# A hybrid decoder step on one Trainium2 core: RWKV preparation in a written-out pipeline, compression copies on GpSimd, the feed-forward program of TensorE without its loop

## What is computed

```python
def rwkv7_mix(xr, wkv0, lw):              # xr: token-shifted projection, p + (previous p - p) * mu
    r, k, v = xr[..., :o1], xr[..., o1:o2], xr[..., o2:o3]
    wl, al, gl = xr[..., o3:o4], xr[..., o4:o5], xr[..., o5:]
    w_log = -jax.nn.softplus(-(lw['w0'] + jnp.tanh(wl) @ lw['w2']).astype(f32)) - 0.5
    decay = jnp.exp(-jnp.exp(w_log))
    a = jax.nn.sigmoid((lw['a0'] + al @ lw['a2']).astype(f32))
    g = jax.nn.sigmoid(gl) @ lw['g2']
    kk = heads(k * lw['k_k'])
    kk = kk / jnp.maximum(jnp.sqrt(jnp.sum(kk * kk, axis=-1, keepdims=True)), 1e-12)
    kf = heads(k * (1.0 + (a - 1.0) * lw['k_a']))
    ...                                   # the recurrence uses r, decay, kf, v, kk, kk * a
    bonus = jnp.sum(rf * kf * lw['r_k'].astype(f32).reshape(H_R, HEAD_DIM_R), axis=-1, keepdims=True) * vf

def compress(rows, lw):                   # rows of the cache in chunks of 16, two chunks to a block
    part = jnp.einsum('bcjehd,esjdf->bcsehf', chunks, w1.reshape(2, R, D_CMP, HEAD_DIM, PHI_HIDDEN))
    h = sum(part[:, s:s + n_blk, s] for s in range(R)) + pe_term
    return jnp.einsum('bcehf,efd->bcehd', jax.nn.silu(h), lw['phi_w2'])

def channel_mix(x, lw):
    h = rms_norm(x, lw['g_ffn'])
    return x + (jax.nn.silu(h @ lw['w_gate']) * (h @ lw['w_up'])) @ lw['w_down']
```

## Time and profile before

| what | value |
|---|---|
| median of 3 runs | 4073.5 us (4072.82 to 4081.59) |
| the profiled execution | 4076.17 us |
| its span, first to last instruction | 4074.6 us |
| busy: PE, DVE, ACT, Pool | 86%, 39%, 25%, 8% |
| RWKV preparation, first DMA to the next stage's first DMA | 687.8 to 875.3 us |
| compression, first DMA to the next stage's first DMA | 1229.3 to 1709.4 us |
| feed-forward, first split of its input to the last add | 2494 to 4046 us |

### The profile page before, as it was taken

How to read it: one execution, slowest core, us unless ns; L and a number is a source line. 1 busy time by engine, 2 the same in 40 slices (tenths; PEclk the granted TensorE clock), 3 DMA queues, 4 the chain that set the end, 5 groups by cost and what they waited for, 6 DMA issues and landing times. The chain is left out here.

```text
span 4074.6 us, 69658 instructions
## 1 busy us (share of the span) xinstructions
PE 3508.3 (86%) x29755; PEld 3159.1 (78%) x29755; DVE 1577.7 (39%) x1995; ACT 1029.8 (25%) x1362; POOL 317.8 (8%) x454
## 2 busy tenths in 40 slices
PE   5999997559945888754599898999999999999998
PEld 5999996348834666632433698999999999999997
DVE  3222221953364777421255423333333333333334
ACT  4112110423213555200133323122112211211212
POOL 1000000223510000020000000000000000000000
PEclk8999996569977999787699999999999999999999
DMA  5334321344605433162300232323323332333232
GB/s 163 107 113 117 101 81 30 118 138 124 155 27 213 167 161 139 32 143 65 123 20 11 63 88 73 93 84 94 94 90 87 94 91 88 92 94 92 86 94 94
DMA packets 504916, 401.53 MB, mean 99 GB/s; under 512 B 148339, under 2 KB 457729, under 8 KB 500033
## 3 DMA queue, kind: packets, MB, share of 16 engines
q1 hardware_dynamic: 458752, 276.11, 24.4%
q0 software_dynamic: 14816, 113.89, 7.5%
q10 hardware_dynamic: 31104, 7.88, 0.9%
HBM read 359.36 MB, written 50.02 MB: 100 GB/s over the span
## 5 line engine op out<-in xcount | busy, mean ns | idle before, releaser
L2453 DVE TENSOR_TENSOR f_w_lo<-wo_raw,f_w_hi 128x2048 fp32r<-128x2048 f32 x132 | 302.5, 2292 | 820.4 <-ACT f_w_hi L2425 820.4
L53 PE MATMUL d_ps<-hh,f_w_hi 128*128 128x260 f32 x2816 | 568.4, 283 | 28.0 <-DVE xt L2477 16.3
L57 PE MATMUL d_ps<-hh,f_w_lo 128*128 128x260 f32 x2816 | 568.4, 284 | 0.0
L55 PE MATMUL d_ps<-hl,f_w_hi 128*128 128x260 f32 x2816 | 567.4, 283 | 0.0
L2425 ACT CAST f_w_hi<-wo_raw 128x2048 fp32r<-128x2048 f32 x132 | 251.9, 1908 | 994.6 <-DMA wo_raw<-in_w_gate 389.0
L53 PEld LDWEIGHTS d_ps<-hh,f_w_hi 128*128 128x128 f32 x2816 | 435.1, 189 | 30.2 <-issue 18.1
L57 PEld LDWEIGHTS d_ps<-hh,f_w_lo 128*128 128x128 f32 x2816 | 435.1, 189 | 0.0
L55 PEld LDWEIGHTS d_ps<-hl,f_w_hi 128*128 128x128 f32 x2816 | 433.8, 189 | 0.0
L53 PE MATMUL d_ps<-f_hid_hi,f_w_hi 128*128 128x260 f32 x1408 | 283.5, 282 | 0.0
L57 PE MATMUL d_ps<-f_hid_hi,f_w_lo 128*128 128x260 f32 x1408 | 283.4, 282 | 0.0
L55 PE MATMUL d_ps<-f_hid_lo,f_w_hi 128*128 128x260 f32 x1408 | 282.4, 282 | 0.0
(11 more groups left out here) (427 smaller groups left out, 5950.3 us busy)
## 6 DMA issues: line engine op xcount, KB each, us to landing
p_w<-in_w_in SPq DMA_DIRECT2D x46, 1024.0 KB, 5.6
wo_raw<-in_w_gate SPq DMA_DIRECT2D x44, 1024.0 KB, 5.6
wo_raw<-in_w_up SPq DMA_DIRECT2D x44, 1024.0 KB, 5.9
wo_raw<-in_w_down SPq DMA_DIRECT2D x44, 1024.0 KB, 5.0
wo_raw<-in_w_o SPq DMA_DIRECT2D x16, 1024.0 KB, 6.1
rk_chunks<-r_outb POOLq DMA_DIRECT2D x8, 1280.0 KB, 5.7
s_cur<-rk_chunks SPq DMA_DIRECT2D x8, 1280.0 KB, 7.1
s_one_vecs<-samp_rows SPq DMA_DIRECT2D x80, 128.0 KB, 4.9
```

The costliest lines, as they stand in the source:

```text
L53: pe.matmul(out[j], w_hi, x_hi[j], start=start, stop=False)
L55: pe.matmul(out[j], w_hi, x_lo[j], start=False, stop=False)
L57: last = pe.matmul(out[j], w_lo, x_hi[j], start=False, stop=stop)
L2453: dve.tensor_tensor(w_lo[:, s, :], w_raw[:, s, :], w_hi[:, s, :].bitcast(F32), ALU.subtract).then_inc(lo_done, 1)
```

## The change

Three stages are changed; the others stay as they are.

1. RWKV preparation: written out for the 8 pairs, with two buffers for most tiles. The token shift becomes x * (1 - mu) on ACT (in place, with the scale in `om`) and one instruction on DVE that adds mu times the row before, which a DMA now loads as a second copy shifted by one column (`prv`, `k_prev`, `lprv`). Keys of all pairs are loaded and shifted ahead of the pairs. The norms are made for all pairs at once: a product with `sel` collects the sums of squares of 16 heads on 16 partitions, one square root and one reciprocal follow, and a product with `spread` gives them back to the 128 partitions of a pair. The factor of the decay moves into the scale of the exponentials. Pool gains the second running sum (`inner`), `bvec` and a further factor of `outb`. Parameters are loaded as rows and turned by PE.
2. Compression: all copies of `arrange` are on Pool, in its own program, and the refill of a half follows its copies there.
3. Feed-forward: PE's loop over the parts is written out.

```diff
 # stage_rwkv_prep, SP
-                with sp.Fori(0, NPAIR) as i:
-                    sp.wait_ge(z_done, i * 3)
-                    sp.wait_ge(x_ready, i)
-                    for j in range(3):
-                        sp.dma_start(raw[:, j, 1:], g.proj_t[bass.ds(i * P + j * D_R, P), :]).then_inc(raw_in, 16)
-                    ...
+                for n in range(2):
+                    qs = slice(4 * n, 4 * n + 4)
+                    sp.dma_start(k_all[:, qs, :], by_pair[:, 1, qs, 0:TC]).then_inc(k_in[n], 16)
+                    sp.dma_start(k_prev[:, qs, 1:SEQ], by_pair[:, 1, qs, 0:SEQ - 1]).then_inc(k_in[n], 16)
+                    ...
+                for q in range(NPAIR):
+                    s = q % 2
+                    if q >= 2:
+                        sp.wait_ge(x_ready, q - 1)
+                    sp.dma_start(raw[:, s], by_pair[:, 0:3:2, q, 0:TC]).then_inc(rv_in[s], 16)
+                    sp.dma_start(prv[:, s, :, 1:SEQ], by_pair[:, 0:3:2, q, 0:SEQ - 1]).then_inc(rv_in[s], 16)
+                    ...
 # Pool
+                def inner(q):
+                    ...
+                    pool.tensor_tensor(cum[:, s, 1, :], cum[:, s, 0, :], sw[:, s, 0:SEQ], ALU.subtract).then_inc(cum1_ready, 1)
+                inner(0)
+                for q in range(NPAIR):
+                    s = q % 2
+                    if q + 1 < NPAIR:
+                        inner(q + 1)
+                    pool.wait_ge(kkn_ready, q + 1)
+                    pool.tensor_tensor(bvec[:, s, :], kkn[:, s, :], a[:, s, :], ALU.mult).then_inc(bvec_done, 1)
+                    pool.wait_ge(exp_done, q + 1)
+                    ...
+                    pool.tensor_tensor(o[:, :, 1, :], chunks(xr[:, s, 0, 0:SEQ]), e0, ALU.mult)
+                    pool.tensor_copy(o[:, :, 2, :], chunks(xr[:, s, 1, 0:SEQ]))
+                    pool.tensor_tensor(o[:, :, 4, :], chunks(kf[:, s, 0:SEQ]), e1, ALU.mult)
+                    pool.wait_ge(bvec_done, q + 1)
+                    pool.tensor_copy(samp[:, q, 2, :], bvec[:, s, SEQ:TC])
+                    pool.tensor_tensor(o[:, :, 3, :], chunks(bvec[:, s, 0:SEQ]), e1, ALU.mult).then_inc(pool_out, 1)
+                    pool.wait_ge(pool_out, q + 1)
+                    pool.wait_ge(out_ready, q + 1)
+                    pool.dma_start(g.rk_chunks[:, :, q, :].rearrange("c p n -> p c n"), ...).then_inc(stored[s], 16)
 # PE
+                for q in range(NPAIR):
+                    pe.wait_ge(sq_ready, q + 1)
+                    for h in range(2):
+                        last = pe.matmul(ps[0:16, 6 + h, 0:HC], sel[:, q, :], sq[:, q % 2, h * HC:(h + 1) * HC], ...)
+                    last.then_inc(ss_done, 1)
+                for q in range(NPAIR):
+                    if q + 1 < NPAIR:
+                        lift(q + 1)                 # the six small products of the next pair
+                    pe.wait_ge(nrm_ready, 1)
+                    ...                             # two with spread, two for the bonus of pair q
 # ACT
+                scale_k(0)
+                act.wait_ge(lora_ready, 3)
+                ...                                 # tanh, copy, sigmoid of the small inputs
+                scale_k(1)
+                scale_rv(0)
+                sigmoids(0)
+                ...                                 # the eight squares, then one square root
+                for q in range(NPAIR):
+                    if q + 1 < NPAIR:
+                        scale_rv(q + 1)
+                        sigmoids(q + 1)
+                    exps(q)
 # DVE
+                def shift(q):
+                    s = q % 2
+                    if q >= 2:
+                        dve.wait_ge(pool_out, q - 1)
+                        dve.wait_ge(out_ready, q - 1)
+                    dve.wait_ge(rv_scaled, 2 * q + 2)
+                    ...                             # two scalar_tensor_tensor of 520 into xr
+                def keys(q):
+                    ...                             # the scan, two steps of kf, rkk
+                def finish(q):
+                    ...                             # kkn, the bonus, small copies, one factor of outb
+                shift(0)
+                keys(0)
+                dve.wait_ge(root_ready, 1)
+                step(dve.tensor_scalar(nrm[:, 0, :], nrm[:, 0, :], 1e-12, None, ALU.max))
+                dve.reciprocal(nrm[:, 1, :], nrm[:, 0, :]).then_inc(nrm_ready, 1)
+                for q in range(NPAIR):
+                    if q + 1 < NPAIR:
+                        shift(q + 1)
+                        keys(q + 1)
+                    finish(q)
 # stage_compress, Pool
+                def arrange(i, half, w=P, start=False):
+                    for e in range(2):
+                        ...
+                        if not start:
+                            pool.wait_ge(turned, i * T + JP * (2 * half + e - 1))
+                        pool.tensor_copy(kvr[0:w, e], kv[0:w, half, :, e * 256:e * 256 + 256].rearrange(
+                            "p j (h d) -> p h j d", h=4)).then_inc(arranged[e], 1)
-                        for e in range(2):
-                            pool.wait_ge(arranged[e], i * 2 + h + 1)
-                        load(i * 2 + 2 + h, h, i * 2 + 3 + h)
+                        arrange(i, h)
+                        refill(i, h)
 # stage_compress, ACT and DVE: every arrange(act.copy, ...) and arrange(dve.tensor_copy, ...) is taken out
-                        if n == 2 * JP + 2 and halves == 2:
-                            arrange(act.copy, act, i, 1, 1, w)
-                        if q == 4 and u == 1 and halves == 2:
-                            arrange(dve.tensor_copy, dve, i, 1, 0, w)
 # stage_ffn, PE
-                part(0, True)
-                with pe.Fori(1, PARTS) as i:
-                    part(i, False)
+                for i in range(PARTS):
+                    part(i, i == 0)
```

More of the change, by code:

```diff
@@ new lines, in stage_rwkv_prep @@
+        x_ready, rkk_ready, cum_ready, cum1_ready, exp_done = (sem(n) for n in (
+            "x_ready", "rkk_ready", "cum_ready", "cum1_ready", "exp_done"))
+        bc_done, bonus_done, kkn_ready, bonus_used, bvec_done, out_ready, pool_out = (sem(n) for n in (
+            "bc_done", "bonus_done", "kkn_ready", "bonus_used", "bvec_done", "out_ready", "pool_out"))
+        chain, rows_turned, rows_copied, rows_out = sem("chain"), sem("rows_turned"), sem("rows_copied"), sem("rows_out")
+        stored = [sem(f"stored{n}") for n in range(2)]
@@ new lines, in _, with lift @@
+                pe.transpose(ps[:, 4, 0:NV], vrow[:], g.ident[0:NV, 0:NV]).then_inc(vec_turned, 1)
+                def lift(q):
+                    for j, bank in enumerate((0, 2, 0)):
+                        if j == 2:
+                            pe.wait_ge(sw_ready, q + 1)
+                        elif q:
+                            pe.wait_ge(gate_ready if j == 0 else a_ready, q)
+                        for h in range(2):
+                            last = pe.matmul(ps[:, bank + h, 0:HC], lw[span[j], j, q * P:(q + 1) * P],
+                                             lora[span[j], j, h * HC:(h + 1) * HC], start=True, stop=True)
+                        last.then_inc(z_done, 1)
@@ new lines, in _, with scale_k @@
+                act.wait_ge(om_ready, 1)
+                act.wait_ge(lraw_in, 16 * 9)
+                for j in range(3):
+                    act.activation(lraw[span[j], j, :], lraw[span[j], j, :], ACT.Copy,
+                                   scale=om[span[j], 64 + j:65 + j]).then_inc(l_scaled, 1)
+                def scale_k(n):
+                    act.wait_ge(k_in[n], 48)
+                    for q in range(4 * n, 4 * n + 4):
+                        act.activation(k_all[:, q, :], k_all[:, q, :], ACT.Copy, scale=om[:, 8 + q:9 + q]).then_inc(k_scaled, 1)
@@ new lines, in _ @@
+                dve.wait_ge(vec_turned, 1)
+                dve.tensor_copy(vec[:], ps[:, 4, 0:NV]).then_inc(vec_ready, 1)
+                dve.wait_ge(vec_ready, 1)
+                dve.tensor_scalar(om[:], vec[:], -1.0, 1.0, ALU.mult, ALU.add).then_inc(om_ready, 1)
+                dve.wait_ge(edge_ready, 3)
+                for j in range(3):
+                    dve.wait_ge(l_scaled, j + 1)
+                    dve.scalar_tensor_tensor(out=lora[span[j], j, :], in0=lprv[span[j], j, :], scalar=vec[span[j], 64 + j:65 + j],
+                                             in1=lraw[span[j], j, :], op0=ALU.mult, op1=ALU.add).then_inc(lora_ready, 1)
```

392 lines of the change are left out of this document (210 added, 182 removed).

## The result

The changed kernel takes 3987.2 us (median; 3984.1 to 3997.0) against 4073.2 us before: a ratio of 0.978, interval 0.977 to 0.980, 86 us less where 56 were forecast, and 0.8 us below the stated range. Between the two profiled executions the spans differ by more, 92.2 us (4074.6 and 3982.4).

| stage | before | after | difference | forecast |
|---|---|---|---|---|
| preparation | 187.4 | 150.1 | -37.3 | -22 |
| chunks (not edited) | 272.8 | 263.1 | -9.7 | 0 |
| compression | 477.2 | 454.1 | -23.1 | -22 |
| two stages behind it (not edited) | 237.2 + 325.3 | 234.2 + 322.0 | -6.3 | 0 |
| feed-forward | 1553.8 | 1537.1 | -16.7 | -12 |

The account below looks back on a forecast made before the run. With TensorE busy 86% of the span, time was taken to be lost where it is not. Gains of 22 (preparation), 22 (compression) and 12 (feed-forward), 56 us, off the median of 4073.5 gave 4017.5 us; 8-in-10 range 3988 to 4044.

Parts of the forecast that it names:

- the start of the preparation: Preparation: keys, squares, norm products, root and reciprocal come before the first pair, with the norms ready at +62.3 us.
- The period of 12.5 us a pair: Preparation: a chain through VectorE and Pool of 11.1 us, plus contention, sets each pair; bounds 11.1 and 14.
- Rival A: Preparation: busiest engine sets the pace, 9.7 us a pair and keys sooner, 20 to 25 us more off, 3995; chance 0.20.
- Rival C: Preparation: contention between Pool and VectorE sets the pair, 14 us or more, with a late start, 4040; chance 0.12.
- 22 us forecast: Compression: gain from moving copies to Pool, 17 of stalls plus 7 of clock less 2 for the first copy.
- the stalls of 0.8: Compression: TensorE's stalls behind the old copies; two go and one shrinks by 0.5 in each sample, 17 us.
- The clock's part: Compression: four of five falls of the granted clock behind stalls were counted as gone, 7 us.
- the bound of 25: Compression: upper bound of the gain in us, with all five falls of the clock gone.
- Rival D: Compression: Pool's copy sets the pace, kernel slower than before; 4074 at 13.7 us a copy, 4115 at 15; chance 0.04.
- The cover: Compression: each Pool copy but the first is hidden under a whole unit of 12.6 us.
- the 12 us of the forecast: Feed-forward: gain from writing out TensorE's loop, out of 16.3 us of stalls at ten boundaries; bounds 0 and 16.
- the add's hold: Feed-forward: TensorE's wait for VectorE's add, some 0.3 to 0.4 us at each boundary, expected to stay.

Follow-up runs that it names:

- e15_norms_twice: The changed kernel with the preparation's 16 products for the norms each made a second time: 4001.8 us, ratio 0.982 to the kernel before.
- e4_three: The changed kernel with three instead of two buffers for the preparation's r, v and kf tiles: 3991.2 us, ratio 0.979 to the kernel before.
- e2_compress: The kernel before with the new compression stage alone: 4050.6 us, ratio 0.993.
- e1_prep: The kernel before with the new preparation stage alone: 4090.6 us, ratio 1.003.
- e7_four: The changed kernel with each of Pool's copies in compression made four times: 4134.6 us, ratio 1.014 to the kernel before.
- e3_ffn: The kernel before with TensorE's written-out feed-forward program alone: 4069.6 us, ratio 0.997.
- e8_prep_shifted: e1_prep with 64 idle instructions ahead of TensorE's feed-forward loop: 4042.4 us, ratio 0.992 to the kernel before.
- e10_loop_kept: The changed kernel with the feed-forward stage, and so TensorE's loop, of the kernel before: 4066.2 us, ratio 0.998.
- e11_before_half: The kernel before with 62 idle instructions ahead of TensorE's feed-forward loop: 4107.6 us, ratio 1.007.
- e13_small: e4_three with five 8-column copies of each preparation pair moved from VectorE to ScalarE: 3989.8 us, ratio 0.979 to the kernel before.

## Why the prediction was wrong

Between the two profiles the forecast missed 36 us of gain: 15 in the preparation, 10 in the chunk stage, 6 in the two stages behind compression, 5 in the feed-forward and 1 in compression, less 1 in the gaps. Two steps failed by most: the start of the preparation was priced too long, and stages that are not edited had no term at all.

**The sum had no term for stages that are not edited.** The prediction added up the three edited stages and gave the others nothing, not even width. The chunk stage brought 9.7 us in the profiled pair, 6 to 7 in the mean of the kernels, through the place of TensorE's program alone. The stall was in the trace of before, named "issue", and no row was read there. The prediction also took straight code to be free of such stalls, which the chunk stage is not. With 6 us of width the range would have held the time. A further 6.3 us of the difference between the two profiles stand in two stages which vary by as much between kernels that don't touch them (233.2 to 238.9 and 322.0 to 325.5 us); they belong to no step.

**Preparation: the mechanism right, the start mis-sized.** The period of 12.5 us a pair was 12.27, with the shift waiting for Pool as said. The end came 150.1 us behind the first DMA instead of 165.1. Of these 15 us, 13 are the start, with the norms there at +49 instead of +62: the second half of the keys was there at +27 instead of +35 (the DMA moved 334 GB/s from 700 to 714 us, where the one large transfer of the earlier trace rows gives 207), and the norm products took 9.0 us instead of 15.5, since the clock rose; ScalarE's work between the two took 8.3 us instead of 6. The first two stood in the prediction as bounds; e15_norms_twice shows that the products count in full. Rival A was nearer in time and wrong in its reason: no pair went at 9.7, and e4_three shows that loosening the chain doesn't lead there. Rival C's contention is real. On the chain of after it hit one step of `kf` on VectorE (1.65 us for 0.70) and Pool's small copy (0.65 for the 0.2 that was taken): 1.4 us, as much as was priced, though not on Pool's product; the other instructions that it hit lie beside the chain.

**Compression: right, a little low.** 22 us forecast, 23 between the profiles and 24 in e2_compress; the stalls of 0.8 are gone and those of `keep_part` are left. The clock's part is not steady: of the five falls of 3.4 us in before two are left in after and one in e2_compress, where e1_prep with the old copies has seven. In the mean the stage takes 479.5 us in the seven kernels with the old copies and 452.9 in the seven with the new ones as they are, 26.6 apart, just past the bound of 25. Pool's copy takes 3.61 us, the lower end and the value by columns from the memset; 4 was taken. The Trainium skill, GPSIMD Engine Reference, § 4.1 Engine selection, sends elementwise work to VectorE but puts one-input work on Pool at roughly line rate. Pool was the slower engine for this copy, 3.61 against VectorE's 2.28 us; it costs nothing under a cover of some 10.6. Rival D put the cover at 12.6 and 15 us a copy at 4115; e7_four with 14.9 took 4134.6. The cover was read from the old sample, which was longer by the stalls that the change removes, and it left out that two copies and a refill of 2.2 us share Pool's queue.

**Feed-forward: the step held alone, the condition was missed.** On the kernel before the gain was the 12 us of the forecast, with 2.7 us of the add's hold left at the boundaries and 1.8 inside parts. In after it was 16.7, because VectorE's add was through in time: the split ahead of it ended 1.6 to 1.8 us before the last product at every boundary (at 2704.56 at one of them), in e3_ffn 0.5 to 1.75 us. What makes the split earlier there than in e3_ffn was not tested. That TensorE waited for the loop rather than for the add is confirmed by e3_ffn, and by the heads of e8_prep_shifted, which pause with the add long over. But a branch's price was taken from the trace as if it were fixed. It depends on what stands ahead of the loop, and the same change lengthened that: with the new preparation the loop would have cost 61 us more (e1_prep, e10_loop_kept). Had the change left the loop in place, the forecast of its other two parts, 44 us, would have met a gain of about 10. That the sum of three parts came as near as it did is luck in this respect: the third part took away a loss that the first would have caused, and the prediction saw neither.

## What to carry to other kernels

When an edit changes the length of an engine's program, everything behind it moves against the blocks in which instructions are fetched: look in all stages, edited or not, for waits put down to "issue", above all behind the head of a loop and in dense runs of short products, and test by moving the code with idle instructions where the engine waits anyway. Do not take a view's releaser for the cause where what it names was over in time. Measure parts together as well as alone: here one part cost 13 us alone and helped once another had removed the loop behind it. Where two engines slow each other, as VectorE and Pool do here, count their common work before loosening a wait between them.

## What the runs showed of the hardware

- A loop's head some 25 instructions ahead of the end of a block cost about 4 us in each pass (e1_prep), at 60 instructions 0.4 to 2.4 us (e11_before_half), at some 120 (the kernel before) nothing, beside transfers of 1 MB at some 300 GB/s. From the last product of a pass to the first product of the block behind the head's were 6.8 to 7.6 us in e1_prep. The head itself came 1.4 to 1.9 us behind the last product in e8_prep_shifted, with all that it waits for over.
- 62 and 97 idle instructions made a kernel of 4075 us slower by 0.7 and 1.5%, and 64 made e1_prep faster by 1.2%.
- The stalls themselves are less than the loss: in e1_prep 35.9 us of stalls went with a loss of 61, and the granted clock of the stage was 0.98 against 1.00.
- VectorE's fused products of 520 columns took 0.65 to 0.76 us alone. Beside Pool's instructions many took 1.10 to 1.76, and `rkk` 2.52 in the mean in e13_small, but some no more than alone (0.68 there, 0.75 in e4_three); what decides between them was not tested. The bonus product, which reads PSUM, took 0.68 to 0.70 us beside Pool in after, e4_three and e13_small alike.
